# A hybrid decoder step in fp32 on one core: MLP products of 448 and 288 columns, with 64 tokens as the stationary operand

## What is computed

```python
z = rmsnorm(x, attn_norm_g) @ w_in
...
h = x + mix @ w_out
y = h + jnp.square(jax.nn.relu(rmsnorm(h, mlp_norm_g) @ w_mlp_up)) @ w_mlp_down   # 2048 -> 8192 -> 2048
```

## Time and profile before

| what | value |
|---|---|
| median of 3 runs | 1184.19 us (1182.78 to 1184.59) |
| the profiled execution | 1184.51 us, its span 1182.7 us |
| TensorE busy | 1174.5 us, 8492 products recorded |
| VectorE, ScalarE, POOL busy | 749.6, 425.8, 139.2 us |
| mean granted TensorE clock | 0.997 of full speed |
| HBM traffic | 191 MB, 162 GB/s over the span |

### The profile page before, as it was taken

The page is one execution under the profiler, slowest core; times in us unless marked ns, Lnnn a source line. Parts: engine busy times, 40 slices in busy tenths (PEclk is TensorE's granted clock), DMA queues, the critical chain, the costliest instruction groups (busy, mean ns, idle before and its releaser), DMA issues.

```text
span 1182.7 us, 20247 instructions
## 1 busy us (share of the span) xinstructions
PE 1174.5 (99%) x8492; PEld 1104.5 (93%) x8492; DVE 749.6 (63%) x754; ACT 425.8 (36%) x515; POOL 139.2 (12%) x83
## 2 busy tenths in 40 slices
PE   9999999999999999999999999999999999999998
PEld 7577576799999999999999999999999999999998
DVE  7899899899776565544555554555564455565454
ACT  6100012975544333333333433333433333433331
POOL 0322512000000000100000110000110000110000
PEclk9899999999999999999999999999999999999999
DMA  7453333534445444454545455554445554445553
GB/s 290 137 140 125 111 115 126 175 122 143 162 157 191 170 161 167 154 178 165 174 161 166 155 178 165 171 164 163 158 152 188 170 168 160 161 148 184 174 171 117
DMA packets 55192, 190.29 MB, mean 161 GB/s; under 512 B 7864, under 2 KB 10168, under 8 KB 54712
## 3 DMA queue, kind: packets, MB, share of 16 engines
q1 hardware_dynamic: 54824, 188.79, 47.9%
q10 hardware_dynamic: 288, 0.30, 0.1%
HBM read 185.82 MB, written 5.28 MB: 162 GB/s over the span
## 4 chain that ended last, share of the span: by engine, by line
PE 94%; DVE 3%; issue 1%; ACT 1%; DMA 0%; SPq 0%
PE psum L1367 94%; DVE states L745 1%; DVE states L933 1%; DVE out_turn L745 0%; DVE turn L745 0%; DVE out_turn L975 0%; PE psum L1486 0%; DMA w_raw<-in_w 0%; ACT gate L606 0%; DVE q_t L993 0%; ACT L531 0%; DVE q_t L745 0%; ACT au L554 0%; DVE carry_p L745 0%; DVE kv_t L1025 0%
## 5 line engine op out<-in xcount | busy, mean ns | idle before, releaser
L736 DVE TENSOR_TENSOR w_lo<-w_raw,w_hi 128x1024 fp32r<-128x1024 f32 x292 | 407.1, 1406 | 385.5 <-ACT w_hi L450 384.7
L1367 PE MATMUL psum<-mov_b,w_hi 128*128 128x288 f32 x2624 | 522.4, 295 | 0.3 <-ACT gate L606 0.3
L450 ACT ACTIVATE w_hi<-w_raw 128x1024 fp32r<-128x1024 f32 x292 | 306.2, 1057 | 481.5 <-PE psum L1367 480.7
L1367 PEld LDWEIGHTS psum<-mov_b,w_hi 128*128 128x128 f32 x2624 | 419.8, 188 | 1.6 <-issue 0.7
L1367 PE MATMUL psum<-mov_a,w_hi 128*128 128x288 f32 x2048 | 406.6, 295 | 0.0
L1367 PE MATMUL psum<-mov_b,w_lo 128*128 128x288 f32 x1312 | 385.4, 294 | 0.0
L1367 PEld LDWEIGHTS psum<-mov_a,w_hi 128*128 128x128 f32 x2048 | 327.7, 188 | 0.1
L1367 PE MATMUL psum<-mov_a,w_lo 128*128 128x288 f32 x1024 | 300.7, 294 | 0.0
L1367 PEld LDWEIGHTS psum<-mov_b,w_lo 128*128 128x128 f32 x1312 | 247.6, 189 | 0.0
L1367 PEld LDWEIGHTS psum<-mov_a,w_lo 128*128 128x128 f32 x1024 | 193.3, 189 | 0.0
L1367 PE MATMUL psum<-x_g,w_raw 128*128 128x288 f32 x640 | 163.9, 414 | 0.3 <-DMA w_raw<-in_w 0.3
(11 more groups left out here) (182 smaller groups left out, 520.3 us busy)
## 6 DMA issues: line engine op xcount, KB each, us to landing
w_raw<-in_w SPq DMA_DIRECT2D x335, 512.0 KB, 3.3
h_t<-in_x SPq DMA_DIRECT2D x3, 576.0 KB, 8.4
out_y<-h_t SPq DMA_DIRECT2D x3, 576.0 KB
b_w<-in_b SPq DMA_DIRECT2D x1, 1024.0 KB, 7.5
c_w<-in_c SPq DMA_DIRECT2D x1, 1024.0 KB, 7.3
k_cache<-in_kc SPq DMA_DIRECT2D x1, 1024.0 KB, 5.8
v_cache<-in_vc SPq DMA_DIRECT2D x1, 1024.0 KB, 7.0
out_kc<-in_kc SPq DMA_DIRECT2D x1, 992.0 KB
```

Source lines behind the costliest of these rows:

```text
L450: nc.scalar.activation(hi3[:, n % SLOTS, :], raw3[:, n % SLOTS, :], ACT.Copy) \
L736: nc.vector.tensor_tensor(lo3[:, n % SLOTS, :], raw3[:, n % SLOTS, :], hi3[:, n % SLOTS, :].bitcast(F32), ALU.subtract) \
L1367: return nc.tensor.matmul(out, lhs_t, rhs, start=start, stop=stop)
```

## The change

The columns of the MLP's work are arranged anew. Of the 288 tokens, 224 (A) and 64 (B) are treated differently. A k-tile's 576 columns now lie as lo of A (224), hi of A (224), hi of B (64), lo of B (64).
- `streams`: per output tile two products: w_hi over the first 448 columns (lo A and hi A, into separate PSUM columns 0 to 447), and w_lo over the 288 columns of hi (into columns 224 to 511). At the first k-tile the w_hi product takes 512 columns.
- `passing`: the 128 columns hi B and lo B are the stationary operand, and the hi weights of all output tiles of the unit (384 or 256 columns) stream past them, into the set's fourth bank. For k = 0 a tile with zeros and lo B (`first_b`) stands in for them.
- `turn_b`: the fourth bank (tokens on partitions) is copied to SBUF and turned by an fp32 product with two stacked 64 x 64 identities, which also adds the two halves, into columns 448 to 511. In up rows this is done for each unit, after the second k-tile of the next one. In down rows VectorE sums the fourth bank over the four blocks in `b_sum`, and it is turned in the last row only.
- Units have 3, 3, 3, 3, 2, 2 output tiles instead of four times 4; six units make a row, eight rows (up and down in turn) the MLP. A step is 2 k-tiles x 384 columns, or 4 k-tiles x 256 columns: 40 a row, 320 in all.
- VectorE adds the two partial sums of A (a copy out of PSUM, an addition, a copy of B), then squares in one operation in up rows; in down rows it adds the fourth bank to `b_sum` and multiplies A and B by r_b apart.
- The sum of squares of h is taken after the fifth unit; the root follows.
- In the head, initial states are turned in two halves: the first before u, the second before the second input rotation. `carry_e` is computed behind u. SP issues the first half step of weights before the small table.

```diff
+TOK_B = 64
+TOK_A = TOK - TOK_B
+UNIT_OUTS = (3, 3, 3, 3, 2, 2)
+UNIT_STEPS = (8, 8, 8, 8, 4, 4)
...
             first = SMALL["h0"].start
+            sp.dma_start(raw4[:, 0, 0, :], ins["w"][0, :, 0:STEP_N]).then_inc(w_first, 16)
             sp.dma_start(small[:, 0:first], ins["small"][:, 0:first]).then_inc(small_loaded, 16)
-            sp.dma_start(raw4[:, 0, 0, :], ins["w"][0, :, 0:STEP_N]).then_inc(w_first, 16)
...
+            def bres_from(u, row, past=0):
+                mlp_unit_full(act, u, row, past)
+                cols = slice(0, UNIT_OUTS[u] * P)
+                nc.scalar.activation(bres[:, cols], mlp_b(u), ACT.Copy).then_inc(bres_out, 1)
...
+            def act_up(row, past=0):
+                for u in range(ROW_UNITS):
+                    hi_ahead(u, row, past, SLOTS + 1 - UNIT_STEPS[u], SLOTS - 1)
+                    bres_from(u, row, past)
+                    hi_ahead(u, row, past, SLOTS - 1, SLOTS + 1)
+                    hid_his(u, row, past)
...
+            one_over_root(UNIT["rms_x"], r_b)
+            turn_h0(0)
+            u = UNIT["g_u0"]
+            unit_full(dve, u)
+            for o in range(4):
+                tt(u3[:, o, :], banks(u)[:, o, :], r_b[:, :], ALU.mult).then_inc(evacuated[u % 2], 1)
...
             y_out(0)
+            turn_h0(1)
             dve.wait_ge(last_copied, 4)
...
+            def low_sum(part, u, row, past):
+                nc.vector.tensor_copy(part[:, :, 0:TOK_A], mlp_outs(u, slice(0, TOK_A))).then_inc(low_copied, 1)
+                dve.wait_ge(low_copied, (2 * past + row) * ROW_UNITS + u + 1)
+                tt(part[:, :, 0:TOK_A], part[:, :, 0:TOK_A], mlp_outs(u, slice(TOK_A, 2 * TOK_A)), ALU.add)
+
+            def up_out(u, row, past=0):
+                lo_ahead(u, row, past, SLOTS + 1 - UNIT_STEPS[u], SLOTS)
+                mlp_unit_full(dve, u, row, past)
+                if u >= 2:
+                    dve.wait_ge(hid_lo, past * ROW_UNITS + row // 2 * ROW_UNITS + u - 1)
+                lo_ahead(u, row, past, SLOTS, SLOTS + 1)
+                part = sr4[:, u % 2, 0:UNIT_OUTS[u], :]
+                dve.wait_ge(b_turned, past * ROW_UNITS + row // 2 * ROW_UNITS + u + 1)
+                low_sum(part, u, row, past)
+                nc.vector.tensor_copy(part[:, :, TOK_A:TOK], mlp_outs(u, slice(2 * TOK_A, 512))) \
+                    .then_inc(mlp_free[(N_UNITS + u) % 2], 1)
+                own_freed(row, u, past)
+                nc.vector.scalar_tensor_tensor(part, part, 0.0, part, ALU.max, ALU.mult).then_inc(hid_ready, 1)
...
+            def streams(u, o, k, w, tile, turned=False):
+                slot, at, out = w
+                w_h, w_l = (t[:, slot, at + o * P:at + (o + 1) * P] for t in (hi3, lo3))
+                cols = 512 if k == 0 else 2 * TOK_A
+                mm(out[:, o, 0:cols], w_h, tile[:, 0:cols], start=k == 0, stop=False)
+                return mm(out[:, o, TOK_A:512], w_l, tile[:, HI], start=False, stop=k == KT - 1 and not turned)
...
+            def passing(row, u, k, w, tile):
+                slot, at, _ = w
+                return mm(mlp_b(u), tile[:, 2 * TOK_A:2 * TOK] if k else first_b[:, row % 2, :], hi3[:, slot, at:at + UNIT_OUTS[u] * P],
+                          start=k == 0, stop=k == KT - 1)
+
+            def turn_b(u, row):
+                if row % 2 == 0:
+                    pe.wait_ge(bres_out, row // 2 * ROW_UNITS + u + 1)
+                    src = bres
+                else:
+                    pe.wait_ge(b_summed, u + 1)
+                    src = b_sum[:, FIRST_OUT[u] * P:(FIRST_OUT[u] + UNIT_OUTS[u]) * P]
+                for o in range(UNIT_OUTS[u]):
+                    done = mm(mlp_outs(u, slice(2 * TOK_A, 512))[:, o, :], src[:, o * P:(o + 1) * P], stack,
+                              start=False, stop=True)
+                done.then_inc(b_turned, 1)
...
+                for k in range(KT):
+                    w, tile = slot_of(u, row, k), mov[:, k, :]
...
+                    for o in range(UNIT_OUTS[u]):
+                        streams(u, o, k, w, tile, turned=row % 2 == 0 or row == ROWS - 1)
+                    done = passing(row, u, k, w, tile)
+                    if k % per == per - 1:
+                        done.then_inc(step_used, 1)
+                    if k == 1 and between:
+                        turn_b(*between)
```

More of the change, by code:

```diff
@@ L76, in steps_at_end @@
 def steps_at_end(unit):
[L78 to L80 removed]
+    return STEPS_AT_END.get(UNITS[unit][0])
 def small_units(unit):
@@ L88, in evacuations, with step_cols @@
 def evacuations(unit):
-    return sum(n for _, n in UNITS[unit % 2:unit + 1:2]) + len(
-        range(N_UNITS + (unit - N_UNITS) % 2, unit + 1, 2))
+    return sum(n for _, n in UNITS[unit % 2:unit + 1:2])
+def step_cols(n):
+    if n < S_MLP or (n - S_MLP) % ROW_STEPS >= FIRST_STEP[4]:
+        return STEP_COLS
+    return STEP_K * UNIT_OUTS[0] * P
 SMALL = {}
@@ L710, in _, with hi_ahead @@
-            with act.Fori(0, N_BLOCKS - 1) as b:
-                for g in range(4):
-                    mlp_hi(4 + g, b)
-                for g in range(4):
-                    mlp_hi(8 + g, b)
-                    relu_part(g, b, before=4)
-            for g in range(4):
-                mlp_hi(4 + g, N_BLOCKS - 1, last=g == 3)
+            def hi_ahead(u, row, past, first, last):
+                end = S_MLP + row * ROW_STEPS + FIRST_STEP[u] + UNIT_STEPS[u]
+                hi_parts(range(max(end + first, S_MLP + SLOTS), min(end + last, N_STEPS)), past)
@@ L720, in _, with act_down @@
+            def act_down(row, past=0):
+                for u in range(ROW_UNITS):
+                    hi_ahead(u, row, past, SLOTS + 1 - UNIT_STEPS[u], SLOTS + 1)
+            hi_parts(range(S_MLP + SLOTS, S_MLP + SLOTS + 1))
+            act_up(0)
+            with act.Fori(0, N_BLOCKS - 1) as b:
+                act_down(1, b)
+                act_up(2, b)
+            act_down(ROWS - 1)
         @block.vector
@@ L1295, in _, with lo_ahead, own_freed @@
-            mlp_lo(7, N_BLOCKS - 1, last=True)
-            dve.wait_ge(added, 4 * (N_BLOCKS - 1) + 2)
-            for o in range(OUTS):
+            def lo_ahead(u, row, past, first, last):
+                end = S_MLP + row * ROW_STEPS + FIRST_STEP[u] + UNIT_STEPS[u]
+                lo_parts(range(max(end + first, S_MLP + SLOTS), min(end + last, N_STEPS)), past)
+            def own_freed(row, u, past):
+                dve.wait_ge(mlp_free[(N_UNITS + u) % 2], past * ROW_UNITS + mlp_freed(row, u))
@@ L1298, in _ @@
+            for u in range(ROW_UNITS - 1):
+                down_out(u, ROWS - 1, last=True)
+            u = ROW_UNITS - 1
+            cols = slice(14 * P, 16 * P)
+            dve.wait_ge(b_last, 1)
+            tt(b_sum[:, cols], b_sum[:, cols], mlp_b(u), ALU.add).then_inc(b_summed, 1)
+            dve.wait_ge(added, ROW_UNITS * (N_BLOCKS - 1) + 4)
+            for o in range(2):
                 dve.wait_ge(last_full, o + 1)
-                link(tt(tb4[:, 1, o, :], banks(N_UNITS + 3)[:, o, :], r_b[:, :], ALU.mult))
+                part, out = tb4[:, 1, o, :], psum[:, mlp_bank(u) + o, :]
+                link(nc.vector.tensor_copy(part[:, 0:TOK_A], out[:, 0:TOK_A]))
@@ new lines, in _ @@
+            unturned = None
+            for row in range(ROWS):
+                for u in range(ROW_UNITS):
+                    if row == ROWS - 1 and u == ROW_UNITS - 1:
+                        last_unit(row, u, unturned)
+                        continue
+                    mlp_unit(row, u, unturned)
+                    unturned = (u, row) if row % 2 == 0 or row == ROWS - 1 else None
+                    if row == 0 and u == 4:
+                        pe.wait_ge(h_summed, 4)
+                        mm(psum[:, mlp_bank(4) + 2, 0:TOK], ones, ssq[:, :], start=True).then_inc(h_sum_full, 1)
```

365 lines of the change are left out of this document (213 added, 152 removed).

## The result

The changed kernel takes **1210.2 us** (median of 4 runs, 1209.1 to 1214.2) where the kernel before took 1184.1 beside it: a ratio of 1.0236, 95% interval 1.0221 to 1.0252. It is **slower by 2.4%**; 1173.4 was forecast, and 1184 was the upper end of the range. The profiled execution took 1210.38 us, its span 1208.6, 25.9 us more than the span of before.

The account below looks back on a forecast made before the run. TensorE, 99% busy, was taken to bound the kernel in one unbroken 912 us piece of products. -35.7 + 3.4 + 21.2 + 3.9 + 0.8 - 4.4 = -10.8 us from the median 1184.19 gave 1173.4 us, range 1164 to 1184.

Parts of the forecast that it names:

- the 12.2 ns: MLP products: 132.2 ns per 288-column product less 120 ns of streaming at 2.4 GHz; read as a floor set by weight load.
- Part 1: MLP products: fewer and wider, 7 instead of 9 per k-tile of three output tiles, columns unchanged; -35.7 us.
- floor of 132.2 ns: Each warm fp32r product: least time, set by its weight load, hiding streaming up to 288 columns; wider ones stream at 2.4 GHz.
- Only columns count: Rival, all products: streaming plus 3 ns each, 1193.1 us; if the whole 132.2 ns goes by column, 1209; chance 0.03.
- surcharge per product: Rival, fp32r products: 12.2 ns goes with each, so 1280 fewer save 15.6 us, giving 1193.5 us; chance 0.10.
- late splits: Rival, even-row units: splits delayed beyond 1.3 us of cover stall 24 units; 1180.6 to 1192.6 us; chance 0.10.
- Cheap turns: Rival, turning the sums: fp32 turns take 109 ns a record or less, 1169.6 down to 1161 us; chance 0.08.
- Part 2: First k-tile of each output: streams 512 columns instead of 448, 27 ns x 128, +3.4 us.
- Part 3: Turning the sums: 80 fp32 products, two records each at 132.2 ns, +21.2 us; changing between fp32r and fp32 free.
- Part 4: MLP waits: TensorE waits for sums in the last row, +3.9 us; even-row splits have 1.3 us of cover.
- Part 5: Kernel end: the last tile takes a copy, an addition, two products and a final addition, about 1.7 against 1.0, +0.8 us.
- Part 6: Head: TensorE resumes earlier near 37 us, idle 0.6 us, no clock fall; -4.4 us; SP's order taken as nothing.

Follow-up runs that it names:

- bench2: Kernel before with other series of 32 products behind its end (fewer rows, small stationary operands, bf16): 448 bf16 columns 189 ns, 64-column products 32 to 58 ns.
- turn_one: Changed kernel with one fp32 product a turn instead of three or two: 1200.7 us, ratio 1.0159 to the kernel before.
- head_sp: Kernel before with halved states, carry factors behind u and SP's new order of first transfers: 1183.7 us, ratio 1.0004.
- head: Kernel before with only the halved initial states and the carry factors behind u, SP's order unchanged: 1181.3 us, ratio 0.9987.
- bench: Kernel before with series of equal products, 64 to 512 columns wide, behind its last store, other engines idle: 112 ns up to 224 columns, 132 for 288, 207 for 448.
- bench3: Kernel before with series behind its end, without 64-column products, varying rows, stationary tiles and banks: 448 fp32r columns 202 to 203 ns, 207 with 32 rows.
- narrow256: Kernel before with MLP products behind each output's first k-tile over 256 of 288 columns: 1101.8 us, ratio 0.9317.
- head_again: The program of head run once more, on another chip: 1181.2 us, ratio 0.9985 to the kernel before.

## Why the prediction was wrong

**The step that failed is the reading of the 12.2 ns, and with it Part 1.** "Streaming only hides once it is longer" was put as a floor of 132.2 ns with 0.417 ns a column above it. The runs show about 0.459 ns for every fp32r column from 256 on (0.459 and 0.460 in the kernels' own steps, 0.445 to 0.468 in the series), at every row count, with idle engines and with zeros, and a load floor of 112 ns that 288 columns (132 ns) covered already. So widening from 288 to 448 columns hid nothing; 2592 columns a k-tile stayed 2592, and -35.7 us became +1.7. That term alone is 37.4 us off, and forecast and result lie 36.8 apart: the errors of the others cancel.

**How the evidence misled.** The earlier trace rows ran at half clock, where 288 columns take 240 ns; what the mode adds is some 12 ns at full clock and nothing at half (448 columns 373 ns in bench2). The earlier trace rows is another mode: 243 ns an fp32 record, twice 0.421 a column, say nothing of fp32r. And the earlier trace rows gave durations of the loads, whose slope was right for the load, but a load plus "about 28 ns" was fitted to the pace that it was to explain. In the whole trace stood one warm width of fp32r, and one point cannot tell a floor from a slope. A law in width was extrapolated from it, for a change whose every gain was that law.

**The rivals.** "Only columns count" was right in its second form, "if the whole 132.2 ns goes by the column, 1209": the result is 1210.2. That the numbers meet so closely is part luck: the 1209 keeps the turns at 21.2, though the sentence says that they too go by the column (some 9 us, and 1197 in all); they stand on the load's floor, 17.7, and the head gave less than the 4.4. It had part of 0.03 and deserved about as much as the forecast. The surcharge per product falls by the k-tiles (1.165 us; 1.193 measured) and by 448 columns (199 ns; 202 to 207 measured), and so do late splits: TensorE waited for w_lo once, 0.6 us, at the MLP's start, and never in the even rows. Cheap turns were right, at 111 ns a record, but had no gain left to add to. The prediction named its own refutation, 199 ns for 448 columns; it came worse.

**Part 2** was right but for the price of a column (3.8 against 3.4). **Part 3** put the record at 132.2 ns, the same wrong floor; it is 111, 17.7 us instead of 21.2. Changing between fp32 and fp32r cost nothing, as said. **Part 4** was right: two long waits of 3.2 us in sum, short ones of about 0.2 (the turn behind the product at 1115.60 starts at 1115.95, 0.17 after its turn), and the splits' cover of 1.3 us held. **Part 5** was right within 0.1 us.

**Part 6** was right in that the clock then stays at 1.00. Its idle time of 0.60 us came out as forecast, but by luck: the changed kernel's first projection ended 2 us late, after the slow start. In turn_one and head_sp, with the same order of SP and no slow start, TensorE idled 1.32 and 1.35 us. Two sizes were off. The order of SP, "taken as nothing; bounds -0.4 and +0.5", costs 1.0 us in the traces and 2.4 in the median (head_sp against head): the small table, not the weights, was what ScalarE's first operand and VectorE's whole queue waited for. And the 2.6 us of the clock stood in the one profile read, not in every execution of before. By the shortest executions the head gives 1.1 us without SP's order (1180.6 against 1181.7) and 0.2 with it (1181.45), not 4.4.

**Open.** Why the fp32r mode streams at 0.459 ns a column was not found; only that rows, data, stationary columns, banks and neighbours don't change it much. Whether it belongs to the mode or to its 4-byte columns, which bf16 has not, no run separates. 384 columns at 0.452 and 512 at 0.445 in bench stand off the line, and the same 448 columns took 203 and 207 ns in two runs. Why the clock rose late in two executions and fell near 262 us in four is not known. Single executions of the changed kernel and of turn_one at a mean clock of 0.997 (1214.2 and 1202.9 us) have no trace, so where the clock fell in them is unknown.

## What to carry to other kernels

Before a change that trades many narrow products for fewer wide ones, count the streamed columns: where they stay and the pace already lies over the load's floor, there is nothing to gain, and every turn, copy and wait that the rearrangement needs is a loss. A price per product, per column or a floor cannot be told apart from one width; several widths in the same mode, at the same clock and in the kernel's own mix can (here 256, 288, 320 and 384 columns in a row of equal products would still have allowed a price per product), and a row of another mode or of half the clock is no witness. For the first microseconds, look at who waits for which transfer before swapping two of them, the queues behind the first operand included, and compare many executions, not two traces.

## What the runs showed of the hardware that was not expected

- fp32r products stream at about 0.459 ns a column at full granted clock (0.452 to 0.468 from 256 to 448 columns), bf16 ones at 0.417 plus 2.5 ns, an fp32 product in two records of 0.84 a column each. At half clock fp32r takes 0.833 a column, 448 columns 373 ns (bench2), with no surplus.
- The pace of a product has a floor that grows with its stationary columns: 32 ns for 32, 58 for 64, 112 for 128 (fp32r, and for 128 fp32 alike). The Trainium skill (TensorE: Matmul & The Clock Gate, "LDWEIGHTS (loading the stationary operand)") gives columns / 1.2, 107 ns for 128: close, and visible here as a pace some 5 ns above it.
- The granted clock fell to 0.50 with TensorE never idle: in bench3 at 1203.9 us, after products over 64 rows and then 32 rows had run since 1193.3, and it came back near 1214.2, with full-height products from 1209.0. In bench2 the same followed 64-column products, from 1191.6 to 1222.3.
- In all five traces with the head of before (its untraced executions of 1181.7 us with a mean clock of 1.000 show no such loss), TensorE idled 1.67 to 2.41 us near 39 us and the clock fell to 0.50 for some 3 to 7 us behind it. In the six with an idle time of 0.60 to 1.35 us there it stayed at 1.00.
- In four of the eleven traces (bench, narrow256, head_sp, head_again) the clock also fell to 0.50 for 3.4 us near 262 us, with TensorE busy throughout, just behind two sets of 32 products of 16 columns. It cost 1.5 us. The other seven, with the same products, did not have it.
- The half pace of the start ended between 4.8 and 7.2 us in nine traces, at 9.4 us in the changed kernel and at 10.7 in head_again, the one with SP's new order and the other with the old; the stretches of the profile print a granted clock of 1.00 there all the same.
